# Attention stage of a hybrid encoder block: the order of small products and softmax steps on four engines

## The reference, cut to what matters

```python
h = rms_norm(x, g_mix)
p = h @ w_in                 # queries, keys, values, mLSTM inputs, gates
# group A: sliding-window attention, 8 query heads, 2 kv heads, head width 64, chunks of 64
aq = rms_norm(aq per head, q_norm_gain); ak = rms_norm(ak per head, k_norm_gain)
scores = (q . k) * 64**-0.5 + bias(distance)       # 64 queries x 128 keys of two chunks
probs = softmax(concat([scores, sink]))[..., :-1]
att = probs @ v
# group B: mLSTM in chunks -> mh
mix = concat([rms_norm(att, g_attn_out), rms_norm(mh, g_mlstm_out)])
x = x + mix @ w_out
x = x + (silu(h2 @ w_gate) * (h2 @ w_up)) @ w_down # h2 = rms_norm(x, g_ffn)
```

## Time and profile before

| what | value |
|---|---|
| median of 3 runs | 1057.17 us (1054.38 to 1057.29) |
| profiled execution, first to last instruction | 1054.7 us |
| TensorE matmuls busy | 1027.4 us, 97% of the span |
| VectorE, ScalarE, GpSimd busy | 681.3, 429.8, 706.4 us |
| mean granted TensorE clock | 0.992 |
| TensorE's share of the chain that ended last | 85% |

### The profile page before, as it was taken

The page is one execution under the profiler, slowest core; times in us unless marked ns, Lnnn a source line. Parts: engine busy times, 40 slices in busy tenths (PEclk is TensorE's granted clock), DMA queues, the critical chain, the costliest instruction groups (busy, mean ns, idle before and its releaser), DMA issues.

```text
span 1054.7 us, 13511 instructions
## 1 busy us (share of the span) xinstructions
PE 1027.4 (97%) x4970; PEld 839.6 (80%) x4970; DVE 681.3 (65%) x790; ACT 429.8 (41%) x895; POOL 706.4 (67%) x555
## 2 busy tenths in 40 slices
PE   9999999999999988999999999999999999999978
PEld 7898878878878876878888888888888888888866
DVE  4259359857852579574847676675748576766386
ACT  7545124357640556533434252433334341434420
POOL 0138578825655337977778687787877786886873
PEclk9999999999999998999999999999999999999999
DMA  7223211131032001211121211221121111112104
GB/s 229 58 61 89 71 41 61 61 130 32 23 119 60 21 11 40 68 46 57 53 58 51 60 54 48 60 60 47 53 61 50 58 53 54 57 50 61 54 26 160
DMA packets 71161, 66.06 MB, mean 63 GB/s; under 512 B 5304, under 2 KB 53688, under 8 KB 71096
## 3 DMA queue, kind: packets, MB, share of 16 engines
q1 hardware_dynamic: 70104, 64.71, 19.9%
q10 hardware_dynamic: 992, 0.49, 0.2%
HBM read 60.48 MB, written 4.21 MB: 61 GB/s over the span
## 4 chain that ended last, share of the span: by engine, by line
PE 85%; DVE 6%; ACT 3%; issue 2%; POOL 2%; DMA 0%; POOLq 0%; SPq 0%; DVEq 0%
PE banks L738 27%; PE banks L739 26%; PE banks L740 26%; ACT prob L1370 1%; PE banks L758 1%; PE banks L824 1%; DVE af_lo L1884 1%; DVE prob L1807 1%; POOL wr_lo L677 1%; PE banks L893 1%; DVE smx L1812 1%; PE banks L830 1%; PE banks L918 0%; DVE hf_raw L1539 0%; POOL prob L636 0%
## 5 line engine op out<-in xcount | busy, mean ns | idle before, releaser
L677 POOL TENSOR_TENSOR wr_lo<-wr_raw,wr_hi 128x512 fp32r<-128x512 f32 x231 | 316.1, 1400 | 47.8 <-ACT wr_hi L1200 42.7
L671 POOL TENSOR_TENSOR wr_raw<-wr_raw,wr_raw 128x512 f32<-128x512 f32 x132 | 189.2, 1444 | 124.9 <-DMA wr_raw<-in_w_gate 45.3
L738 PE MATMUL banks<-hf_hi,wr_hi 128*128 128x512 f32 x616 | 244.0, 396 | 5.9 <-issue 3.6
L739 PE MATMUL banks<-hf_lo,wr_hi 128*128 128x512 f32 x616 | 243.5, 395 | 0.0
L740 PE MATMUL banks<-hf_hi,wr_lo 128*128 128x512 f32 x616 | 243.4, 395 | 0.0
L1962 DVE TENSOR_TENSOR x<-banks,x 128x1024 f32<-128x1024 f32 x154 | 187.7, 1223 | 59.6 <-PE banks L740 53.8
L1200 ACT ACTIVATE wr_hi<-wr_raw 128x512 fp32r<-128x512 f32 x231 | 134.7, 624 | 140.5 <-POOL wr_raw L671 138.2
L738 PE MATMUL banks<-w_hi,actT_hi 128*128 128x512 f32 (+1 forms) x448 | 173.1, 386 | 1.5 <-DVE x L1771 1.5
L740 PE MATMUL banks<-w_hi,actT_lo 128*128 128x512 f32 (+1 forms) x448 | 168.6, 376 | 0.0
L739 PE MATMUL banks<-w_lo,actT_hi 128*128 128x512 f32 (+1 forms) x448 | 168.4, 376 | 0.0
L738 PEld LDWEIGHTS banks<-hf_hi,wr_hi 128*128 128x128 f32 x616 | 116.2, 189 | 35.0 <-issue 4.4
(11 more groups left out here) (201 smaller groups left out, 1232.2 us busy)
## 6 DMA issues: line engine op xcount, KB each, us to landing
wr_raw<-in_w_up SPq DMA_DIRECT2D x46, 256.0 KB, 2.9
wr_raw<-in_w_gate SPq DMA_DIRECT2D x44, 256.0 KB, 2.9
wr_raw<-in_w_down SPq DMA_DIRECT2D x44, 256.0 KB, 2.6
w_raw<-in_w_in SPq DMA_DIRECT2D x32, 256.0 KB, 3.5
w_raw<-in_w_out SPq DMA_DIRECT2D x16, 256.0 KB, 2.7
x<-in_x SPq DMA_DIRECT2D x8, 512.0 KB, 6.3
out<-x SPq DMA_DIRECT2D x16, 256.0 KB, 2.2
x_in<-in_x SPq DMA_DIRECT2D x7, 512.0 KB, 4.5
```

Source lines behind the costliest of these rows:

```text
L671: nc.gpsimd.tensor_tensor(wr_raw[slot(q, f)][:, :], wr_raw[slot(q, a)][:, :], wr_raw[slot(q, b)][:, :], ALU.subtract).then_inc(wsum, 1)
L677: nc.gpsimd.tensor_tensor(wr_lo[s][:, :], wr_raw[s][:, :], wr_hi[s][:, :].bitcast(F32), ALU.subtract).then_inc(wf_lo, 1)
L738: nc.tensor.matmul(ps, x_hi, wh, start=first, stop=False, skip_group_check=more)
L739: nc.tensor.matmul(ps, x_hi, wl, start=False, stop=False, skip_group_check=more)
```

## The change

In the loop of each engine, steps change places; no operation on data is added or removed.
- TensorE: `att_scores(s-2)` is put ahead of `att_transposes(s-1)`. `att_sumsq` leaves the end of the slot. It is now called in the middle of the unit, for tile U - 37: in `unit` before step k = 4, in `out_unit` between its two halves. So the sum of tile t stands in the middle of unit 37 + t, where it stood behind that unit before. Its wait for bank 3 is for one tile less (t + 4), and the transposes wait for the copy of one sum more (t - 3).
- ScalarE: the exponentials (s-2) come before the inverse root of the query sums (s) and before the squares and the high part of the attention output (s-4).
- VectorE: the copy of the sum of squares, then the bias addition and maximum (s-2) come first; then query sums, low part of mh, pT, the end of the softmax (s-2), and behind it the normalised queries (s) and the low part of the attention output (s-4).
- GpSimd: `normalise` (s-2) comes before `add_squares` (s-4).

```diff
--- before.py
+++ after.py
@@ -658,10 +658,10 @@
                 split((g * K + n % K) % RING, n % RAW, NKV if g == 1 else N, n, cols[:, c:c + 1])
                 if g == 4:
                     exponents(n % K)
+                if 0 <= n - 4 * K - 2 < T:
+                    normalise(n - 4 * K - 2)
                 if 0 <= n - 4 * K - 4 < T:
                     add_squares(n - 4 * K - 4)
-                if 0 <= n - 4 * K - 2 < T:
-                    normalise(n - 4 * K - 2)
 
             def block_sum(q, f, a, b):
 
@@ -764,6 +764,7 @@
 
                 g, t = U // T, U % T
                 width = NKV if g == 1 else N
+                squares = U - 4 * T - 5
                 ps = bank[U % 2][:, 0:width]
                 if U >= 2:
                     pe.wait_ge(acc_free[U % 2], U // 2)
@@ -772,6 +773,8 @@
                         pe.wait_ge(h_split, 2 * t + k // 4 + 1)
                     if U == 0 and k == K // 2:
                         transpose_tile(x_in, 1, h_tp)
+                    if k == K // 2 and 0 <= squares < T:
+                        att_sumsq(squares)
                     if t == 0:
 
                         if g == 0:
@@ -843,7 +846,7 @@
                 pe.wait_ge(sqa_added, t + 1)
                 if t >= 1:
                     pe.wait_ge(ssa_ready, t)
-                pe.wait_ge(mixb_ready, min(t + 5, T))
+                pe.wait_ge(mixb_ready, min(t + 4, T))
                 nc.tensor.matmul(bank[3][:, 0:1], sqb[:, 0:P], ones[:, 0:1], start=True,
                                  stop=True).then_inc(ssa_mm, 1)
 
@@ -859,8 +862,8 @@
                 last.then_inc(q_tp, 1)
                 if t >= 1:
                     pe.wait_ge(mixb_ready, t)
-                if t >= 5:
-                    pe.wait_ge(ssa_ready, t - 4)
+                if t >= 4:
+                    pe.wait_ge(ssa_ready, t - 3)
                 for kk in range(4):
                     last = nc.tensor.transpose(bank[3][:, kk * P:(kk + 1) * P],
                                                mh[:, t, kk * P:(kk + 1) * P], ident[:, :])
@@ -923,10 +926,13 @@
 
                 j = U - UNITS
                 g, t = U // T, U % T
+                squares = U - 4 * T - 5
                 pe.wait_ge(mixa_ready, t + 1)
                 pe.wait_ge(mixb_ready, t + 1)
                 a = slice(t % 4 * P, (t % 4 + 1) * P)
                 for part, done in ((0, wa_done), (1, wb_done)):
+                    if part == 1 and 0 <= squares < T:
+                        att_sumsq(squares)
                     if j == 0:
                         pe.wait_ge(acc_free[part], UNITS // 2)
                     else:
@@ -1006,14 +1012,12 @@
                 if s == 1:
                     pe.wait_ge(c_ready, T)
                     pe.wait_ge(mh_ready, T)
+                if 0 <= s - 2 < T:
+                    att_scores(s - 2)
                 if 0 <= s - 1 < T:
                     att_transposes(s - 1)
-                if 0 <= s - 2 < T:
-                    att_scores(s - 2)
                 if 0 <= s - 3 < T:
                     att_prob_transposes(s - 3)
-                if 0 <= s - 5 < T:
-                    att_sumsq(s - 5)
                 if 0 <= s - 4 < T:
                     att_values(s - 4)
                 s = U - 6 * T
@@ -1339,11 +1343,6 @@
                     nc.scalar.activation(actT_hi[:, tt // 4, 4:8, tt % 4 * P:(tt % 4 + 1) * P],
                                          bank[3][:, :].rearrange("p (k n) -> p k n", k=4),
                                          ACT.Copy).then_inc(mixb_hi, 1)
-                if 0 <= s < T:
-                    act.wait_ge(q_stat, s + 1)
-                    if s >= 1:
-                        act.wait_ge(qn_ready, s)
-                    inverse_root(qrs[:, :], qss[:, :], HD).then_inc(q_rs, 1)
                 if 0 <= s - 3 < T:
                     tt = s - 3
                     act.wait_ge(pt_done, tt + 1)
@@ -1351,15 +1350,6 @@
                         act.wait_ge(pv_done, tt - 1)
                     nc.scalar.activation(pT[tt % 2][:, 0:4, :], bank[6][:, :].rearrange("p (k n) -> p k n", k=4),
                                          ACT.Copy).then_inc(pTa, 1)
-                if 0 <= s - 4 < T:
-                    tt = s - 4
-                    act.wait_ge(pv_done, tt + 1)
-                    if tt >= 1:
-                        act.wait_ge(ssa_mm, tt)
-                    nc.scalar.activation(sqb[:, :], bank[2][:, :], ACT.Square).then_inc(sqa_done, 1)
-                    nc.scalar.activation(actT_hi[:, tt // 4, 0:4, tt % 4 * P:(tt % 4 + 1) * P],
-                                         bank[2][:, :].rearrange("p (k n) -> p k n", k=4),
-                                         ACT.Copy).then_inc(mixa_hi, 1)
                 if 0 <= s - 2 < T:
                     tt = s - 2
                     act.wait_ge(s_max, tt + 1)
@@ -1370,6 +1360,20 @@
                         step(nc.scalar.activation(prob[tt % 2][:, j, :], prob[tt % 2][:, j, :], ACT.Exp, bias=nmx[:, j:j + 1],
                                                   accum_out=dsum[:, j:j + 1]))
                     nc.scalar.activation(esk[:, :], esk[:, :], ACT.Exp).then_inc(p_exp, 1)
+                if 0 <= s < T:
+                    act.wait_ge(q_stat, s + 1)
+                    if s >= 1:
+                        act.wait_ge(qn_ready, s)
+                    inverse_root(qrs[:, :], qss[:, :], HD).then_inc(q_rs, 1)
+                if 0 <= s - 4 < T:
+                    tt = s - 4
+                    act.wait_ge(pv_done, tt + 1)
+                    if tt >= 1:
+                        act.wait_ge(ssa_mm, tt)
+                    nc.scalar.activation(sqb[:, :], bank[2][:, :], ACT.Square).then_inc(sqa_done, 1)
+                    nc.scalar.activation(actT_hi[:, tt // 4, 0:4, tt % 4 * P:(tt % 4 + 1) * P],
+                                         bank[2][:, :].rearrange("p (k n) -> p k n", k=4),
+                                         ACT.Copy).then_inc(mixa_hi, 1)
                 if 0 <= s - 6 < T:
                     tt = s - 6
                     act.wait_ge(ssa_ready, tt + 1)
@@ -1775,21 +1779,10 @@
                     V_.scalar_tensor_tensor(xs, bank[1][:, :], rmix[:, t, 1:2], xs, ALU.mult,
                                             ALU.add).then_inc(x1_ready, 1)
                 s = U - 4 * T
-                if 0 <= s < T:
-
-                    dve.wait_ge(acc_free[U % 2], U // 2 + 1)
-                    if s >= 1:
-                        dve.wait_ge(q_rs, s)
-                    V_.tensor_reduce(qss[:, :], pq[:, :].rearrange("p (h d) -> p h d", h=HEADS), AX.X,
-                                     ALU.add).then_inc(q_stat, 1)
-                if 0 <= s - 1 < T:
-                    tt = s - 1
-                    dve.wait_ge(mixb_hi, tt + 1)
-                    a = slice(tt % 4 * P, (tt % 4 + 1) * P)
-                    V_.tensor_tensor(actT_lo[:, tt // 4, 4:8, a],
-                                     bank[3][:, :].rearrange("p (k n) -> p k n", k=4),
-                                     actT_hi[:, tt // 4, 4:8, a].bitcast(F32),
-                                     ALU.subtract).then_inc(mixb_ready, 1)
+                if 0 <= s - 5 < T:
+                    tt = s - 5
+                    dve.wait_ge(ssa_mm, tt + 1)
+                    V_.tensor_copy(ss2[:, tt, 0:1], bank[3][:, 0:1]).then_inc(ssa_ready, 1)
                 if 0 <= s - 2 < T:
                     tt = s - 2
 
@@ -1813,10 +1806,37 @@
                     link(V_.tensor_tensor(smx[:, :], smx[:, :], sink_b[:, :], ALU.max))
                     link(V_.tensor_scalar(nmx[:, :], smx[:, :], -1.0, None, ALU.mult))
                     V_.tensor_tensor(esk[:, :], sink_b[:, :], nmx[:, :], ALU.add).then_inc(s_max, 1)
-                if 0 <= s - 5 < T:
-                    tt = s - 5
-                    dve.wait_ge(ssa_mm, tt + 1)
-                    V_.tensor_copy(ss2[:, tt, 0:1], bank[3][:, 0:1]).then_inc(ssa_ready, 1)
+                if 0 <= s < T:
+
+                    dve.wait_ge(acc_free[U % 2], U // 2 + 1)
+                    if s >= 1:
+                        dve.wait_ge(q_rs, s)
+                    V_.tensor_reduce(qss[:, :], pq[:, :].rearrange("p (h d) -> p h d", h=HEADS), AX.X,
+                                     ALU.add).then_inc(q_stat, 1)
+                if 0 <= s - 1 < T:
+                    tt = s - 1
+                    dve.wait_ge(mixb_hi, tt + 1)
+                    a = slice(tt % 4 * P, (tt % 4 + 1) * P)
+                    V_.tensor_tensor(actT_lo[:, tt // 4, 4:8, a],
+                                     bank[3][:, :].rearrange("p (k n) -> p k n", k=4),
+                                     actT_hi[:, tt // 4, 4:8, a].bitcast(F32),
+                                     ALU.subtract).then_inc(mixb_ready, 1)
+                if 0 <= s - 3 < T:
+                    tt = s - 3
+                    dve.wait_ge(pt_done, tt + 1)
+                    if tt >= 2:
```

(28 more changed lines are left out.)

## The result

The changed kernel takes 1095.86 us (median of 4 runs, 1094.78 to 1096.66), the kernel before beside it 1057.23 us: ratio 1.0372, 95% interval 1.0357 to 1.0387. It is slower, as forecast, but by 38.6 us instead of 26.7, and outside the range that reached to 1091. The profiled execution of the changed kernel has a span of 1094.9 us against 1054.7.

The account below looks back on a forecast made before the run. TensorE is busy nearly throughout, so only gaps and lower-clock stretches cost time. First slots -2.7, six slots +32.8, last slot -3.4: +26.7 us on the 1054.7 us span gives 1081.4, plus 2.5 to the median: 1083.9 us, range 1072 to 1091.

Parts of the forecast that it names:

- The place and number of the waits: TensorE waits 3.9 us for GpSimd's folded squares mid-unit, six times, in units 37 to 42; none for tiles 6 and 7.
- The clock: Behind each of the six waits, matmuls run at 1.2 GHz: 1.6 us charged per slot, bounds 0 and 2.4 us.
- The rule of the Trainium skill: A loop waiting for its operand every turn restarts at the lower clock every turn: clock term in all six slots.
- The softmax chain and the additions: From scores' start: bias addition at 1.15 us, 6.98 us to GpSimd's normalisation, its end at 9.67, additions done at 10.95.
- a wait of 0.7 us for the queries in slot 3: On TensorE before the query transposes of slot 3, behind VectorE's normalised queries: one new wait of 0.7 us.
- The prediction's other end of the chain: Softmax chain of 7.79 us, as in slot 9 beside GpSimd's split: 0.8 us a slot more, 5 us in all.
- the clock's bound: Clock cost of 0 to 2.4 us behind each of six waits, giving 1074.3 to 1088.7 us.
- The first slots and the last: Slot 4 starts at 239.9, 2.7 us gained; slot 10 has no wait and its unit ends at 341.2, -3.4 us.
- The rival that ended on the other side: Additions ready when TensorE reaches mid-unit; all listed gaps and two clock falls go: 1048.7 us, chance 0.04.
- the hoped 8.5: Attention-stage gaps of 5.3 us and two clock falls of 3.2 us that would go if the squares came in time.

Follow-up runs that it names:

- experiment 5: Changed kernel with 19 needless matmuls of 512 columns ahead of each of the six waits for the squares: 1081.17 us, ratio 1.0228.
- experiment 2: Changed kernel with GpSimd's old order alone, the additions of the squares before the normalisation: 1086.24 us, ratio 1.0265.
- experiment 3: Changed kernel with ScalarE's old order alone, squares and high part of the attention output ahead of the exponentials: 1096.27 us, ratio 1.0372.
- experiment 6: Changed kernel with 10 needless matmuls instead of 19 ahead of each of the six waits for the squares: 1089.4 us, ratio 1.0296.
- experiment 1: Changed kernel with the sum of squares one unit later, in the middle of unit 38+t: 1057.76 us, ratio 1.0003.
- Experiment 8: Changed kernel with the squares' old order on ScalarE and GpSimd, and VectorE normalising both halves of the probabilities, GpSimd none: 1063.19 us, ratio 1.0054.
- experiments 1 and 4: The first has its own line; the second is the changed kernel with the squares' old order on both ScalarE and GpSimd: 1056.86 us, ratio 1.0003.
- experiment 7: Changed kernel with the squares' old order on ScalarE and GpSimd, and VectorE's queries and low part ahead of its wait for the exponentials: 1054.38 us.

## Why the prediction was right in its mechanism and wrong in its size

**The place and number of the waits: right.** Six waits for GpSimd's sqb in units 37 to 42, none for tiles 6 and 7; TensorE arrives at 7.06 us (7.03 worked out). The old waits for probabilities are gone. The list of the softmax in slot 6, VectorE, ScalarE and GpSimd:

```profile
279.26 1.29 DVE L1800 TENSOR_TENSOR prob<-banks,bias 128x512 f32<-128x512 f32 x2 [6.34 <-PE banks L885]
...
281.85 0.17 DVE L1806 TENSOR_TENSOR smx<-smx,sink_b 128x8 f32<-128x8 f32 x1
...
285.77 0.17 DVE L1834 TENSOR_TENSOR dsum<-dsum,esk 128x8 f32<-128x8 f32 x1 [1.56 <-ACT esk L1362]
...
286.21 0.69 DVE L1838 TENSOR_TENSOR prob<-prob,dsum 128x512 f32<-128x512 f32 x1
286.82 1.53 DVE L1845 TENSOR_TENSOR qn<-aq,qrs 128x512 f32<-128x512 f32 x1
288.28 0.68 DVE L1853 TENSOR_TENSOR actT_lo<-banks,actT_hi 128x512 fp32r<-128x512 f32 x1
```

```profile
282.45 0.40 ACT L1360 ACTIVATE prob<-prob,nmx 128x128 f32<-128x128 f32 x1 [0.76 <-DVE esk L1808]
...
286.08 0.58 ACT L1373 ACTIVATE sqb<-banks 128x512 f32<-128x512 f32 x1
```

```profile
286.26 1.55 POOL L636 TENSOR_TENSOR prob<-prob,dsum 128x512 f32<-128x512 f32 x1 [10.71 <-DVE dsum L1835]
287.77 1.17 POOL L642 TENSOR_TENSOR sqb<-sqb 128x256 f32<-128x256 f32 x1
289.01 0.45 POOL L645 TENSOR_TENSOR sqb<-sqb 128x128 f32<-128x128 f32 x1
```

From the bias addition to GpSimd's normalisation are 286.26 - 279.26 = 7.00 us (6.98 worked out), and ScalarE starts the squares at 286.08, 8.09 us after the scores' start, so they are done at 8.7 as the prediction had it.

**The clock: the term that was mis-sized.** I charged 1.6 us a slot, for 3.4 us at the low level, and bounded it by 2.4. Measured are 2.6 us (experiment 5), since the low level covers the small product and practically all of the twelve matmuls. The failed step is the length of the low stretch. I carried 3.4 us over from single gaps of the kernel before, of 1.95 and of 4.40 us; behind the six repeated waits the clock stayed low for 6.8 us, 5.4 to 6.5 of them behind the end of the wait. The gap of 4.40 us, near in length, was the right one to look at and still gave the wrong size: there TensorE ran at the full level for 0.8 us behind the gap and at the low one for 3.4. What makes a low stretch long or short stays open. It isn't the length of the wait (experiment 2), and a longer wait needn't cost more at the clock, because more of the stretch can lie in the wait (experiment 3).

With the small product the half unit takes 5.77 us and not 4.60: 6 x 1.17 = 7.0 us of the miss. Of the 1.17 us the clock is 1.0; the rest is the half unit at the full level, 3.17 us where I had 3.00.

The rule of the Trainium skill that I weighed ("TensorE: Matmul & The Clock Gate", "HAM oscillation - how this bites in real kernels": where a long wait comes back on every turn of a loop, every turn starts at the low clock) held for all six slots here. Behind the shorter gaps of experiment 6, 1.8 to 2.7 us, the clock fell three times out of six.

**The softmax chain and the additions: too short.** From the scores' start to the product I had 10.95 us; measured are 13.26 in slot 4, 11.83, 11.53 and 11.52 in slots 5 to 7, 11.08 and 11.06 in the last two: 4.6 us more over the six. Two things make most of it, neither in the sum (the longer addition 4 x 0.45 = 1.8 us, slot 4 another 1.7). About 0.7 us more come from the start: the bias addition begins 1.27 us after the scores where I had 1.15; and 0.3 us from slot 5, whose scores still begin at the low clock. The two are:
- VectorE and GpSimd get in each other's way. The queries (286.82) start beside the normalisation, which ends at 287.81, and take 1.53 us instead of 0.69; the first addition starts at 287.77, beside the queries, and takes 1.17 us instead of 0.74. In the last two slots, which have no queries, the chain is 0.45 us shorter. In the slots of the filled gaps and of experiment 1 the same 1.53 us stand. Experiment 8 shows that they go when GpSimd is idle. The Trainium skill, "SBUF — State Buffer", section "Who interferes with whom", has this as a rule: a VectorE instruction with two inputs in SBUF contends with a GpSimd instruction that reads SBUF, and the one that starts first keeps the other off until it has ended. The trace agrees: the queries end 0.54 us after the normalisation does, about the time that they take alone (0.68), and low parts, which read one input from PSUM, stay at 0.68 us beside GpSimd's addition.
- In slots 3 and 4 VectorE wasn't free. I had a wait of 0.7 us for the queries in slot 3 and none later; measured are 1.65 and 1.25 us. The long queries delay the bias addition behind them: in slot 3 it starts at 233.73, 2.68 us after the scores, in slot 4 at 243.48, 2.27 us after. And there the maximum with the sinks stands beside GpSimd's split. Slot 4, the first with a product to wait for:

```profile
243.48 1.27 DVE L1800 TENSOR_TENSOR prob<-banks,bias 128x512 f32<-128x512 f32 x2
...
246.05 0.91 DVE L1806 TENSOR_TENSOR smx<-smx,sink_b 128x8 f32<-128x8 f32 x1
```

0.91 us for 128x8 values (0.93 in slot 3), 0.17 in slot 6 above. The later start, 1.0 us, and the longer maximum, 0.74 us, are what slot 4 has over slots 6 and 7. The prediction's other end of the chain, 0.8 us a slot, was of the right size for such meetings, but it was taken as a rare case and not added to the clock's bound. The range held each of the two deviations alone; 7.0 and 4.6 us came together. Both bounds added in full, 1088.7 + 5 = 1093.7 us, would still have ended below the 1095.86 measured, because the clock's bound of 2.4 us was too low as well.

**The first slots and the last.** Slot 4 starts at 241.21 instead of 239.9. Of the 1.3 us of difference 0.6 are older than the change's first effect (slot 2 starts 0.6 us later in this execution), and the other 0.7 are what the queries leave: they come 1.0 us later than worked out, and the rest of the slot and the unit take 0.3 us less. Slot 10 to the end of unit 43 takes 354.20 - 346.12 = 8.08 us, worked out 8.0. Sum: 0.6 + 0.7 + 7.0 + 4.6 + 0.1 = 13.0 us over the predicted 26.7 in the spans, 40.2 measured; the rest, 0.5 us, isn't assigned. Between the medians the miss is smaller, 1095.86 - 1083.9 = 12.0 us.

**The rival that ended on the other side** (squares in time, 1048.7 us) was priced wrong too: experiments 1 and 4 bring it about, and the time is that of the kernel before. The prediction counted the waits for probabilities as pure gain. But VectorE's new order puts queries and low part behind the end of the softmax, 3.2 us of work after a wait, one operation of it lengthened by GpSimd, and the query transposes then wait in each steady slot. Moved back (experiment 7), 2.5 us of the hoped 8.5 are gained in the medians, 3.6 in the spans of the two profiled executions (1054.7 and 1051.1). The rest are waits: three for probabilities and one for the copied sum stand in that profile, 4.4 us together, while its clock stays at 1.00 from 230 to 320 us. 3.6 and 4.4 make 8.0 of the 8.5.

## What to carry to other kernels

When a consumer is moved earlier, work out when its producer is ready with the producer's whole queue as the change leaves it: here ScalarE's and GpSimd's new order each made the squares late by themselves, and either the old place of the squares or a product one unit later heals it. Price a repeated wait on TensorE as the wait plus the matmuls behind it at the 1.2 GHz level, with a low stretch of 3.4 us as the low end and one of 6.8 us as the high end, as both were measured here. Add the bounds of independent terms instead of taking them in turn. Before two elementwise steps of VectorE and GpSimd are moved next to each other in time, look at whether both read their inputs from SBUF.

## What the runs showed of the hardware

- A kernel with 114 needless matmuls in its gaps is 14.7 us faster than the same kernel without. The ends of the waits stayed in place and the half units behind them took 3.17 instead of 5.77 us.
- Behind repeated waits of TensorE the granted clock stayed at 0.50 for 6.8 us in all six slots of the changed kernel. In experiment 2 it did so for 6.8 us behind a wait of 3.36 us and for 3.4 us behind one of 3.37. What decides between the two isn't known.
- Gaps of 1.8 to 2.7 us between matmuls were followed by a fall of the clock in three slots and by none in three others within one execution, the longest of them by none. All six gaps of 4.0 to 4.9 us in the changed kernel had one, which began in their last 1.4 us, and all twelve waits of experiments 2 and 3, of 3.0 to 5.1 us, had one in them or right behind them.
- A VectorE operation on 128x8 values took 0.17 us alone, and 0.93 and 1.18 us when a GpSimd operation on SBUF was under way; one on 128x512 values, also with both inputs in SBUF, took 0.69 and 1.53 us. GpSimd's operation is lengthened too, 0.74 to 1.17 us, when it starts while such an operation of VectorE is under way.
